# Augmented rows ahead of the table's evictions, three pieces of an output chunk inside the attention's last steps, group sums behind the next scores

## The reference, cut to what matters

```python
h = x @ w_in[l]
(fq, fk, fv, fgate, cq, ckv, kr, sq, sk, sv, wq, wk, wv) = jnp.split(h, points, axis=-1)
log_f = jax.nn.log_sigmoid(fgate + fox_b_f[l]); cum = jnp.cumsum(log_f, axis=1).transpose(0, 2, 1)
out_a = _causal_softmax_blocks(fq, fk, fv, HEAD_DIM ** -0.5, cum)      # fox: logits + cum[t] - cum[s]
out_b = _mla(cq, ckv, kr, ...)                                         # mla: latents normed by rms
out_c = _stick_breaking_blocks(sq, sk, sv)
out_d = _swa_sink_alibi(wq, wk, wv, swa_sinks[l], slopes)              # window of 128 keys
mix = jnp.concatenate([out_a, out_b, out_c, out_d], axis=-1)
y = _group_rmsnorm(mix, mix_g[l]) @ w_o[l]
x = _layernorm(ALPHA * x + y, ln1_g[l], ln1_b[l])
```

## Time and profile before

| | before |
|---|---|
| median of 3 runs | 3262.15 us (3261.52 to 3265.43) |
| profiled execution: its own time | 3264.54 us |
| its span, first to last instruction | 3262.6 us |
| PE busy | 3193.5 us, 98% of the span |
| mean granted clock of PE | 0.986 of full speed |

### The profile page before, as it was taken

How to read it: one execution, slowest core, us unless ns; L and a number is a source line. 1 busy time by engine, 2 the same in 40 slices (tenths; PEclk the granted TensorE clock), 3 DMA queues, 4 the chain that set the end, 5 groups by cost and what they waited for, 6 DMA issues and landing times.

```text
span 3262.6 us, 43028 instructions
## 1 busy us (share of the span) xinstructions
PE 3193.5 (98%) x15686; PEld 2640.7 (81%) x15686; DVE 1502.8 (46%) x1999; ACT 710.6 (22%) x1452; POOL 1945.3 (60%) x1542
## 2 busy tenths in 40 slices
PE   7999999999989999999999999999999999999998
PEld 6777888887778888878888778888888887788887
DVE  5576332256763232464316774432344238664422
ACT  3453211033532110221102231110111012321100
POOL 3334666645345666477766557776677666277764
PEclk9998999999999999999999999999999999999999
DMA  4111223222112222132223212222222232132221
GB/s 166 58 40 52 97 96 97 93 83 78 46 46 84 97 96 92 64 103 96 97 97 107 72 59 98 96 97 97 96 96 96 97 113 84 46 97 96 96 97 65
DMA packets 83017, 284.08 MB, mean 87 GB/s; under 512 B 9531, under 2 KB 15068, under 8 KB 82652
## 3 DMA queue, kind: packets, MB, share of 16 engines
q1 hardware_dynamic: 77632, 274.76, 25.4%
q10 hardware_dynamic: 5276, 7.73, 0.7%
HBM read 278.79 MB, written 3.67 MB: 87 GB/s over the span
## 4 chain that ended last, share of the span: by engine, by line
PE 73%; issue 13%; POOL 9%; DVE 4%; ACT 1%; DMA 0%; POOLq 0%; SPq 0%; DVEq 0%; ACTq 0%
PE bank_v L506 15%; PE bank_v L508 15%; PE bank_v L507 15%; PE bank_a L506 7%; PE bank_a L508 7%; PE bank_a L507 6%; POOL w_lo L480 5%; POOL w_hi L478 3%; POOL zero L477 1%; PE bank_s L932 1%; PE bank_v L799 1%; PE bank_a L778 1%; PE bank_v L947 1%; DVE mix L2202 0%; PE bank_s L935 0%
## 5 line engine op out<-in xcount | busy, mean ns | idle before, releaser
L480 POOL TENSOR_TENSOR w_lo<-raw,w_hi 128x1024 fp32r<-128x1024 f32 x512 | 1299.0, 2537 | 41.2
L477 POOL TENSOR_TENSOR zero<-zero 128x1 f32<-128x1 f32 x512 | 130.8, 255 | 1244.8 <-PE bank_v L508 896.6
L506 PE MATMUL bank_v<-xn_hi,w_hi 128*128 128x512 f32 (+1 forms) x1696 | 648.7, 382 | 20.2 <-DVE xn_lo L1577 13.2
L508 PE MATMUL bank_v<-xn_hi,w_lo 128*128 128x512 f32 (+1 forms) x1696 | 639.4, 377 | 0.0
L507 PE MATMUL bank_v<-xn_lo,w_hi 128*128 128x512 f32 (+1 forms) x1696 | 639.1, 377 | 0.0
L478 POOL CAST w_hi<-raw 128x1024 fp32r<-128x1024 f32 x512 | 549.4, 1073 | 0.0
L506 PE MATMUL bank_a<-xn_hi,w_hi 128*128 128x512 f32 (+1 forms) x1248 | 478.0, 383 | 16.8 <-DVE xn_lo L1577 6.2
L507 PE MATMUL bank_a<-xn_lo,w_hi 128*128 128x512 f32 (+1 forms) x1248 | 472.7, 379 | 0.0
L508 PE MATMUL bank_a<-xn_hi,w_lo 128*128 128x512 f32 (+1 forms) x1248 | 472.7, 379 | 0.0
L506 PE MATMUL bank_v<-h_hi,w_hi 128*128 128x512 f32 (+1 forms) x1122 | 424.0, 378 | 0.0
L508 PE MATMUL bank_v<-h_hi,w_lo 128*128 128x512 f32 (+1 forms) x1122 | 422.5, 377 | 0.0
(11 more groups left out here) (371 smaller groups left out, 3358.7 us busy)
## 6 DMA issues: line engine op xcount, KB each, us to landing
raw<-in_w_stream SPq DMA_DIRECT2D x516, 512.0 KB, 3.3
resid<-in_x SPq DMA_DIRECT2D x8, 256.0 KB, 8.2
rope<-in_rope ACTq DMA_DIRECT2D x2, 1024.0 KB, 5.9
da_v<-t_rows ACTq DMA_DIRECT2D x2, 1024.0 KB, 5.8
out<-resid SPq DMA_DIRECT2D x8, 256.0 KB, 2.3
t_rows<-t_row ACTq DMA_DIRECT2D x1, 1536.0 KB, 8.6
mla_v<-in_alibi ACTq DMA_DIRECT2D x2, 512.0 KB, 6.8
work<-in_lru_w ACTq DMA_DIRECT2D x2, 256.0 KB, 2.8
```

Source lines behind the costliest of these rows:

```text
L477: pool.tensor_tensor(zero[:, 1:2], zero[:, 0:1], zero[:, 0:1], ALU.add)
L480: pool.tensor_tensor(w_lo[:, u, :], raw[:, u, :], w_hi[:, u, :].bitcast(F32), ALU.subtract).then_inc(*w_split.done(("unit", u)))
L506: pe.matmul(out, lhs_hi, rhs_hi, start=first, stop=False)
L508: return pe.matmul(out, lhs_lo, rhs_hi, start=False, stop=last)
```

## The change

Three edits, all in layer1. (1) In lap 0 DVE writes the augmented rows before it evicts the table's rows, instead of behind them. (2) For output chunk 2 the pieces k=0, 1 and 2 are made inside the attention, one in each of the steps n=32, 33 and 34, ahead of that step's products with values and transposes. For this the bank of that chunk changes from `bank_s[2]` to `bank_s[1]`, ACT's high halves of chunks 0 to 3 move into steps n=29 to 32 (before: chunks 0 and 1 in n=32, 2 and 3 in n=33), and DVE's low halves into n=30 to 33 (before: 0 and 1 in n=34, 2 and 3 in n=35). (3) PE's sums for the stick group move from the end of step 29 to behind the scores of step 30.

```diff
@@ -93,6 +93,7 @@
 OPEN_OUTS = 3
 ROWS_STEP = 27
 APPLY_STEP = 28
+OUTS_IN_STREAM = 3
 OUT_CHUNK = dict(fox=0, mla=2, stick=4, swa=6)
 
 
@@ -368,7 +369,7 @@
         bank_v = [ctx.enter_context(nc.psum_tensor(f"bank_v{i}", [P, S], F32)) for i in range(2)]
         bank_s = [ctx.enter_context(nc.psum_tensor(f"bank_s{i}", [P, S], F32)) for i in range(4)]
         stat_bank = bank_s[3]
-        out_in_scores = bank_s[2]
+        out_in_scores = bank_s[1]
 
         def factor_banks(s):
             return bank_s[1 + s], bank_s[0 if s else 3]
@@ -600,17 +601,20 @@
                     pe.matmul(factor_banks(s)[n][:, HALVES[1]], ones[:, :], work[:, 2 + s, HALVES[n]], start=True, stop=True,
                               skip_group_check=True).then_inc(*sums.done((tag, name, s)))
 
+            def out_chunks(bank, c, ks):
+                u = w_used.slot(("wo", c), SLOTS)
+                for k in ks:
+                    if c == 0 or k < OUTS_IN_STREAM:
+                        pe.wait_ge(*x_lo.after(("mixnorm", k)))
+                    mm = mm3(bank[:, :], *w_tile(u, k), xn_hi[:, k, :], xn_lo[:, k, :], k == 0, k == DC - 1)
+                return mm
+
             def project_out(tag):
 
                 banks = [v_bank(("wo", 0)), None, out_in_scores]
 
                 def chunks(c, ks):
-                    u = w_used.slot(("wo", c), SLOTS)
-                    for k in ks:
-                        if c == 0:
-                            pe.wait_ge(*x_lo.after(("mixnorm", k)))
-                        mm = mm3(banks[c][:, :], *w_tile(u, k), xn_hi[:, k, :], xn_lo[:, k, :], k == 0, k == DC - 1)
-                    return mm
+                    return out_chunks(banks[c], c, ks)
 
                 unit(("wo", 0))
                 chunks(0, range(0, 4))
@@ -621,8 +625,7 @@
                 chunks(0, range(4, 6))
                 chunks(1, range(4, 6))
                 mix_row(3)
-                unit(("wo", 2))
-                chunks(2, range(0, 6))
+                chunks(2, range(OUTS_IN_STREAM, 6))
                 for c in range(OPEN_OUTS):
                     chunks(c, range(6, 8)).then_inc(*w_used.done(("wo", c)))
                 for c in range(OPEN_OUTS, DC - 2):
@@ -907,6 +910,13 @@
                         if i == 0:
                             attention_inputs(tag, p)
                         scores[tag](list(zip(PAIRS[tag][p], s_banks([(tag, h, i) for h in PAIRS[tag][p]]))), i)
+                    if n > 3 * GROUP_ITEMS and group_at(n - 1, 5):
+                        early_sums(group_at(n - 1, 5), added.after((group_at(n - 1, 5), "squares")), group_squares[:, 0, :])
+                    if n == len(STREAM):
+                        unit(("wo", 2))
+                        pe.wait_ge(*s_read.after(("swa", PAIRS["swa"][1][1], TT - 2)))
+                    if 0 <= n - len(STREAM) < OUTS_IN_STREAM:
+                        out_chunks(out_in_scores, 2, (n - len(STREAM),))
                     if pair_ending_at(n - TURN_LAG - 1):
                         pair_values(*pair_ending_at(n - TURN_LAG - 1))
                     filler(n)
@@ -915,7 +925,7 @@
                         tag, p, i = item_at(m)
                         for k, h in enumerate(PAIRS[tag][p]):
                             turn((tag, h, i), probs[:, (2 * m + k) % 8, :], i + 1 - first_block(tag, i))
-                    if group_at(n, 5):
+                    if group_at(n, 5) and n < 3 * GROUP_ITEMS:
                         early_sums(group_at(n, 5), added.after((group_at(n, 5), "squares")), group_squares[:, 0, :])
                     if 0 <= n - ROWS_STEP < EARLY_ROWS:
                         mix_row(n - ROWS_STEP)
@@ -1349,25 +1359,29 @@
                         group_square(group_at(n, 3))
                     if group_at(n, 5):
                         keep_sums(group_at(n, 5), GROUPS.index(group_at(n, 5)))
-                    if n == len(STREAM):
+                    if n == APPLY_STEP + 1:
                         act.wait_ge(*w_used.after(("wq", 1)))
-                        mix_hi_of(0)
+                    if 0 <= n - APPLY_STEP - 1 < 4:
+                        mix_hi_chunk(n - APPLY_STEP - 1)
                     if n == len(STREAM) + 1:
                         mix_root(2, 1)
-                        mix_hi_of(1)
 
             def mix_root(g, groups):
                 cols = slice(g * TT, (g + groups) * TT)
                 act.wait_ge(*dve_step.after(("mix", g, "var")))
                 act.activation(small[:, 16 + cols.start:16 + cols.stop], small[:, cols], ACT.Sqrt).then_inc(*rooted.done(("mix", g)))
 
+            def mix_hi_chunk(c):
+                g = c // 2
+                if c % 2 == 0:
+                    act.wait_ge(*value.after(("mixnorm", c)))
+                else:
+                    act.wait_ge(*(v_read.after(("mixrow", g)) if g < EARLY_ROWS else scaled.after(("mixnorm", c))))
+                split_hi("mixnorm", c, work[:, c % 4, :])
+
             def mix_hi_of(g):
                 for c in (2 * g, 2 * g + 1):
-                    if c % 2 == 0:
-                        act.wait_ge(*value.after(("mixnorm", c)))
-                    else:
-                        act.wait_ge(*(v_read.after(("mixrow", g)) if g < EARLY_ROWS else scaled.after(("mixnorm", c))))
-                    split_hi("mixnorm", c, work[:, c % 4, :])
+                    mix_hi_chunk(c)
 
             act.sem_inc(a_read.sem, 2)
             act.sem_inc(s_read.sem, 4)
@@ -1931,11 +1945,10 @@
                         mix_apply_chunk(n - APPLY_STEP)
                     if n == len(STREAM):
                         mix_variance(2, 1, a_read.after("stick"))
+                    if 0 <= n - APPLY_STEP - 2 < 4:
+                        split_lo("mixnorm", n - APPLY_STEP - 2, work[:, (n - APPLY_STEP - 2) % 4, :])
                     if n == len(STREAM) + 2:
-                        mix_lo_group(0)
                         mix_diagonals(2, 1)
-                    if n == len(STREAM) + 3:
-                        mix_lo_group(1)
                     if pair_ending_at(n - TURN_LAG - 2):
                         tag, p = pair_ending_at(n - TURN_LAG - 2)
                         keep((tag, "out", p), sums, qmix[:, OUT_CHUNK[tag] + p, :])
@@ -2010,17 +2023,17 @@
             dve.wait_ge(*act_step.after("strict_r"))
 
             for l in counts.laps("layer1"):
-                if l == 0:
-                    rows_flat = t5_row[:, :, :].rearrange("p m w -> p (m w)")
-                    for n in range(4):
-                        dve.wait_ge(*sums.after(("t5", n)))
-                        dve.tensor_copy(rows_flat[:, n * S:(n + 1) * S], bank_s[n][:, :]).then_inc(*dve_step.done(("t5", n)))
                 one_hot = ident[0:4, 0:4].unsqueeze(2).to_broadcast([4, 4, S])
                 step(dve.tensor_copy(aug_q[:, :, :], zero[:, 0:1].unsqueeze(2).to_broadcast([P, 4, S])), "aug_zero")
                 step(dve.tensor_copy(aug_k[:, :], zero[:, 0:1].to_broadcast([P, S])), "aug_k0")
                 for r in (0, 64):
                     dve.tensor_copy(aug_k[r:r + 4, :], ones[r:r + 4, 0:1].to_broadcast([4, S]))
                     dve.tensor_copy(aug_q[r + 32:r + 36, :, :], one_hot)
+                if l == 0:
+                    rows_flat = t5_row[:, :, :].rearrange("p m w -> p (m w)")
+                    for n in range(4):
+                        dve.wait_ge(*sums.after(("t5", n)))
+                        dve.tensor_copy(rows_flat[:, n * S:(n + 1) * S], bank_s[n][:, :]).then_inc(*dve_step.done(("t5", n)))
                 dve.wait_ge(*par_in.after("tables1"))
 
                 dve.wait_ge(*w_used.after("kr"))
```

## The result

The changed kernel takes 3242.04 us (median of 4 runs, 3240.15 to 3243.54); the kernel before, on the same chip, 3263.79 (3261.52 to 3266.44). The ratio is 0.9934, its 95% interval 0.9922 to 0.9947: 0.66% less, 21.75 us. I had forecast 14.8 us less, 3247.4, and a range down to 3242.5. The profiled execution took 3243.54 us, span 3241.6, 21.0 less than before.

The account below looks back on a forecast made before the run. PE's own work was taken to bound the kernel; 10.5 us from edit 1 plus 4.3 from edits 2 and 3 over two laps made 14.8 us less, 3247.4 us from the median, range 3242.5 to 3255.5.

Parts of the forecast that it names:

- both terms: Lap 0, PE's wait for DVE's sum of squared latents: 6.97 us of wait and 3.52 of half clock behind it.
- The casts were short: Lap 0 on DVE: augmented-row casts start at 24.99, are short until 31.39, and the first eviction starts at about 40.1.
- a filled wait: Ahead of the stick sums: scores of item 30 fill PE's 1.38 us wait, so a pair's products start 1.4 us earlier.
- moved pieces: Attention tail: three pieces leave the place behind `mix_row(3)`, 2.07 us gone there per lap.
- 0.3 for chunk 6: Behind `mix_row(3)`: PE wants chunk 6 earlier than DVE's low half is ready, about 0.3 us late.
- some 1.0 lost in the stream: Attention tail: 0.65 us for DVE's low half and some 0.35 for piece 2, subtracted from 1.4 us gained.
- The step that failed: Attention tail: edits 2 and 3 together give 2.2 us per lap, 4.3 in two; bounds per lap 1.1 and 3.2.
- the last products 0.4 us earlier: Attention tail: the last products with values start 0.4 us earlier; bounds 1.4 and -0.7.
- my sum: Whole kernel: 10.5 us from edit 1 plus 4.3 from edits 2 and 3, 14.8 us less.
- The tail gives more because PE is not left idle: Rival, 13%: pieces in the tail's gaps keep full clock, 2 us per lap; -19 us in all, 3243.
- The crossing chain: Rival "Slower", 3%: tail pieces, halves, copies and transposes wait on each other, 3.7 us per piece round; 3269.7.

Follow-up runs that it names:

- The run with the stall filled up: Kernel before with 31 thrown-away matmuls of 512 columns in PE's 7.0 us wait ahead of lap 0's latent sums: 3263.05 us, ratio 0.9993.
- the filled norm: Changed kernel plus ten thrown-away 256-column matmuls ahead of each of PE's two waits for DVE's low halves behind a layer norm: 3233.9 us, ratio 0.9904.

## Why the prediction fell short

- **Edit 1** was right in both terms. Forecast 10.5; 10.77 by the second early row, 9 in the run by itself. The casts were short, the eviction came at 39.82, DVE is early by 5 us, nothing took the wait's place. The run with the stall filled up shows the 3.4 of half clock by themselves; the other 7.0 are the wait.
- **Edit 3** as a filled wait was right: no wait of PE ahead of the stick sums, and in lap 0 the products behind them begin 5.40 us after the second early row (225.36 - 219.96) in place of 6.99 (237.72 - 230.73), 1.6 less. In lap 1 it is 2.8, clock included.
- **Edit 2** as moved pieces was about right. I forecast 2.07 gone behind `mix_row(3)`, less 0.3 for chunk 6, and some 1.0 lost in the stream: 0.8. From that row to the shift sum it is 10.22 us after and 11.79 before, 1.6 gone for the 1.8. The last products start 9.33 us behind the first ones; with thrown-away matmuls in place of the pieces it is 8.33, so 1.0 is lost in the stream. Of that 0.6 comes back, because the wait for the row's diagonal is 0.33 and not 0.94.
- **The step that failed** is the clock in the tail. I took the durations of the earlier trace rows as they stood for the forecast, and put the clock into a rival with 13%, at 2 us per lap. Its price left out its largest term. I counted the transposes and the rows of one stretch at half clock, but not its product with values, and not the earlier stretch with the other one: 3.19 and 3.25 us stood in the earlier trace rows side by side, both at 0.50, so the pair looked like one fixed duration. At full clock each is 1.75, 2.9 us per lap together. I forecast the last products 0.4 us earlier behind the second early row; in lap 0 they start 2.6 earlier (14.73 in place of 17.33) and are then 1.5 shorter. Without tail edits the tail measured 42.5 to 44.1 us in eight laps of four kernels (mean 43.4); edit 3 with thrown-away matmuls makes it 38.3. Of these 5.1, 1.4 are the filled wait; the other 3.7, 7.4 in two laps, I put down to the clock, which is an estimate. With them my sum would have been 22.2 us, against 21.0 to 21.75 measured.
- **The rivals.** "The tail gives more because PE is not left idle" is the one that happened, larger than I had priced it. The Trainium skill (TensorE: Matmul & The Clock Gate, "A second HAM failure mode: psum-queue depth-cycling") says that frequent small gaps make the clock swing. The tail of before agrees, with its waits of 1.38, 1.38 and 0.72; but waits of 0.69, 0.21, 0.23 and 0.33 were left in after, and the clock stayed at 1.00. The crossing chain did not form: its links cost 0.21 and 0.23 us.
- **Open:** why the same wait takes the clock down in one execution and not in another (the 2.71 us above), and with it how much of the lead of 23.7 us an execution keeps. The tail is steadier: without tail edits every one of those eight laps has slow products with values, and with them both laps of both profiled executions of the changed kernel have none.

## What to carry to other kernels

When a stretch runs at half clock, price every instruction in it at both clocks before summing, and take the full-clock duration from another lap or another group of the same form; two equal durations side by side prove nothing if both were slow. A PE wait costs itself and can cost clock behind it: 3.4 us behind the 7.0 here, and in the tail some 3.7 in clock for 1.4 of filled wait. So filling it with useful pieces can pay twice, and even matmuls whose result is thrown away can pay when there is nothing useful. Not every wait does this, as the one of 2.71 us shows, so compare the granted clock of the stretch in more than one execution. Look for such waits just ahead of long runs of thin instructions.

## What the runs showed of the hardware

- The clock can fall in a row of one-column sums although PE counts as fully busy: in the filled norm it fell from 0.98 to 0.50 in the middle of 24 of them behind filled waits, and with nine 256-column matmuls among them it stayed at 1.00 in lap 0. It is not certain to fall: sixteen of them behind full work (52.59 in after) did not bring it down, sixteen behind 0.68 us of idle did in the one execution profiled, and 24 in two halves did in lap 0 and not in lap 1.
- What a form costs at a granted clock of 1.00 or of 0.50: 28 products with values 1.75 or 3.25 us, sixteen one-column sums 1.84 or 3.57, four transposes 0.60 or 1.09.
- DVE's cast of 128x2048 takes 1.21 us with POOL idle (24.89 in after) and took 3.36 where POOL had begun a `w_lo` of 2.36 us at 39.84, just ahead of it. Lap 1 of before has both orders. POOL's cast, begun 0.10 us behind DVE's, took 2.04 in place of the 1.03 of other slots, and DVE's cast behind a `w_lo` that POOL began at 717.10 took 3.30:

```profile
714.88 1.24 DVE L2023 CAST aug_q<-ident 4x2048 fp32r<-4x2048 f32 x1
714.98 2.04 POOL L478 CAST w_hi<-raw 128x1024 fp32r<-128x1024 f32 x1
...
717.31 3.30 DVE L2023 CAST aug_q<-ident 4x2048 fp32r<-4x2048 f32 x1
```

  The Trainium skill (SBUF — State Buffer, "Who interferes with whom") speaks of a lock between the two engines; the traces agree with these durations.
